# Ones stationary for row sums, a first root in two parts, ScalarE's high parts ahead of gate copies, and feed-forward matmuls of 512 columns

## The chip, the core and the metric

The kernel runs on one core of a Trainium2 chip. TensorE (PE) multiplies out of SBUF into PSUM, which has 8 banks of 128 partitions by 512 fp32 values; VectorE (DVE) and ScalarE (ACT) do the elementwise work; SyncE (SP) issues the transfers of the weights. Each engine runs its own instructions in order and waits on semaphores for the others. The metric is the device time of one execution in microseconds (us).

## The reference

The network has two blocks of two layers each, on 256 tokens of width 1024, all in fp32. Only what bears on the change is shown.

```python
# first block, layers i = 0 (differential attention with 256 context tokens) and 1 (short convolution)
mod = (silu_c @ ada_w[i] + ada_b[i])[:, None, :]          # 1024 -> 6 * 1024: six "sections" of a layer
sh1, sc1, g1, sh2, sc2, g2 = jnp.split(mod, 6, axis=-1)
h = modulate(rmsnorm(x, norm1_g[i]), sh1, sc1)             # x * (1 + scale) + shift
x = x + g1 * mixer(h)
x = x + g2 * swiglu(modulate(rmsnorm(x, norm2_g[i]), sh2, sc2), ffn_w_in[i], ffn_w_out[i])

def swiglu(t, w_in, w_out):                                # w_in: 1024 x 5632, w_out: 2816 x 1024
    a, b = jnp.split(t @ w_in, 2, axis=-1)
    return (silu(a) * b) @ w_out

# differential attention, per head of 8 (values of width 128), ends with
o = rmsnorm(o, subln_g) * (1.0 - lam_init)                 # over the 128 values of a head
return o.reshape(B, n, D_MODEL) @ wo
```

The second block (neighbourhood attention, then latent attention, each with a gated residual) is computed in the same program. Of it the change moves one instruction of ScalarE.

## The kernel before

**High and low parts.** A product of fp32 accuracy is made of three matmuls of the faster type fp32r: high weights by high input, high weights by low input, low weights by high input. Weights come in units of 1 MB (`raw`, a ring of 3 buffers). For each unit ScalarE rounds `raw` to `high` (`prepare`, L585) and VectorE subtracts to get `low` (`split`, L998). `behind(u)` on either engine makes the parts of unit u + 3: ScalarE's waits until PE is done with unit u (`blocks_done`), VectorE's waits for ScalarE's.

**Feed-forward phases** (`ffn_phase`, one for each layer of the first block). There are 11 steps of 256 hidden features. A step has two feature units (`two_features`, L1710, L1711, L1729), one for a and one for b, and one out unit (`out_unit`, L1625 to L1627) for the hidden features of the step before. The input is `hH`, `hL` (high and low part of x times scale, not yet divided by the root of the mean square), of 256 tokens and 2 columns that hold the shift, so a feature unit is 16 pairs of a 128x258 matmul with `hH` and one with `hL`, and 16 with the low weights. VectorE multiplies the result by `rstd` (`scaled`, L1242); the shift's column is added in ScalarE's silu (L726) and VectorE's `gated` (L1262). Then follow `gH` on ScalarE and `gL` on VectorE, which the next out unit needs.

**Adaptive sections.** The 12 sections of `mod` take rows of `ada_w` times silu(c). The first two are summed on PE (L1811, four column groups of 32 at once) and turned to columns with a selecting matmul (L1828). For the other ten, VectorE accumulates pieces of 128x1024 into `ada_acc` (L977), and PE sums over the partitions with 8 matmuls, `ada_acc` stationary and one column of ones moving (L1648). `reduce_at` holds after which unit each stands. VectorE's `section` then adds the bias. The first stands between two units of the q projection, the next two around the v projection, four in the first feed-forward phase, two in the convolution phase (behind its third and its last feature unit) and one in the second feed-forward phase.

**Attention's end.** Each of 16 (token tile, head) pairs is scored, exponentiated, transposed and multiplied with V; VectorE scales the result into `XN` (L1190) and ScalarE squares it (L691). When all 16 are squared, VectorE makes one root of 16 columns (`inverse_root`), scales four parts of `XN` (L1198), PE transposes them (`output_groups`), ScalarE makes `oH` (L606) and VectorE `oL` (L1045), and only then does the output product (`feature_out`) begin.

**Convolution phase.** Four times three feature units (c, u, g). ScalarE waits for VectorE's `tc`, copies it with its shift to `cg` (L746), and makes the high parts of the next units behind that. In the feed-forward phases silu stands ahead of the high parts in the same way.

## Time and profile before

| what | value |
|---|---|
| three runs | 1091.9, 1090.09, 1090.65 us; median 1090.65 |
| the profiled execution | 1092.87 us |
| its span (first to last instruction) | 1090.8 us |
| mean granted TensorE clock | 0.982 of 2.4 GHz |
| PE matmul busy | 1035.3 us (95%), 7740 instructions |
| DVE busy | 790.3 us (72%) |
| ACT busy | 509.4 us (47%) |
| chain that ended last | PE 79%, DVE 12%, ACT 3% |

Busy time counts a matmul from its start to its modelled end, and successive matmuls overlap; how fast they follow one another is read from their starts. The second block begins near 724 us. The first feed-forward phase runs from about 236 to 430 us, the convolution phase from 436 to 517 us and its output product to 542 us, the second feed-forward phase from there to about 735 us.

### The profile page before, as it was taken

Reading aid. Unit: us, or ns where it says so; the run is one execution under the profiler, and the core shown is the slowest. Engines: PE = TensorE matmul, PEld = TensorE weight load, DVE = VectorE, ACT = ScalarE, POOL = GpSimd, SP = SyncE. Lnnn points to the kernel's source line nnn. Section 1 sums busy time; section 2 is a strip of 40 time slices with the busy share of each in tenths; the row PEclk is TensorE's granted clock in tenths of the full one; section 3 lists DMA queues with packets and bytes.
Section 4 is the critical chain, followed back from the end, with each engine's and each line's share of the span. In section 5 each row is a group of like instructions: output and inputs, shape, how many; then the busy total and the mean of one; then the engine's idle time right before and its main releaser. Section 6 shows DMA issues by size and latency. Waiting matters only on the chain.

```text
span 1090.8 us, 18302 instructions
## 1 busy us (share of the span) xinstructions
PE 1035.3 (95%) x7740; PEld 960.9 (88%) x7740; DVE 790.3 (72%) x1184; ACT 509.4 (47%) x732; POOL 0.7 (0%) x6
## 2 busy tenths in 40 slices
PE   4899999799999999998999999999999999999895
PEld 2689875699999999998999999999987998997684
DVE  3689759668787887887986646568746568896665
ACT  3623238454434344424343444445347665457562
POOL 0000000000000000000000000000000000000000
PEclk9899999899999999999999999999999999999898
DMA  9769541038998987566746676564754053543130
GB/s 367 273 214 330 187 174 39 2 104 291 318 302 293 316 284 245 189 226 233 248 155 209 208 242 213 175 191 129 232 182 162 2 184 119 185 138 150 37 119 38
DMA packets 118592, 210.14 MB, mean 193 GB/s; under 512 B 4250, under 2 KB 82288, under 8 KB 118512
## 3 DMA queue, kind: packets, MB, share of 16 engines
q1 hardware_dynamic: 117764, 206.81, 55.9%
q10 hardware_dynamic: 748, 2.18, 0.5%
q8 instruction: 61, 1.00, 0.4%
q14 instruction: 19, 0.16, 0.1%
HBM read 207.92 MB, written 1.05 MB: 192 GB/s over the span
## 4 chain that ended last, share of the span: by engine, by line
PE 79%; DVE 12%; ACT 3%; issue 2%; DMA 1%; SPq 1%; DVEq 0%; ACTq 0%
PE PS L1625 12%; PE PS L1626 12%; PE PS L1627 12%; PE PS L1710 8%; PE PS L1729 8%; PE PS L1711 8%; DVE low L998 3%; PE PS L1636 3%; PE PS L1748 2%; PE PS L1749 2%; PE PS L1753 2%; PE PS L1843 1%; PE PS L1844 1%; DMA ada_raw<-in_ada_w 1%; PE PS L1916 1%
## 5 line engine op out<-in xcount | busy, mean ns | idle before, releaser
L998 DVE TENSOR_TENSOR low<-raw,high 128x2048 fp32r<-128x2048 f32 (+2 forms) x147 | 328.1, 2233 | 153.5 <-ACT high L585 153.1
L585 ACT ACTIVATE high<-raw 128x2048 fp32r<-128x2048 f32 (+2 forms) x147 | 273.1, 1866 | 226.0 <-PE PS L1627 111.2
L1710 PE MATMUL PS<-hH,high 128*128 128x258 f32 x896 | 221.8, 284 | 4.6 <-ACT high L585 1.9
L1711 PE MATMUL PS<-hL,high 128*128 128x258 f32 x896 | 220.3, 283 | 0.0
L1710 PEld LDWEIGHTS PS<-hH,high 128*128 128x128 f32 x896 | 169.8, 189 | 6.5 <-issue 2.9
L1711 PEld LDWEIGHTS PS<-hL,high 128*128 128x128 f32 x896 | 168.7, 188 | 0.1
L1729 PE MATMUL PS<-hH,low 128*128 128x258 f32 x896 | 126.3, 283 | 0.3
L1729 PEld LDWEIGHTS PS<-hH,low 128*128 128x128 f32 x896 | 115.6, 189 | 1.3 <-DVE low L998 1.3
L1625 PE MATMUL PS<-gH,high 128*128 128x256 f32 x352 | 98.5, 280 | 0.0
L1626 PE MATMUL PS<-gL,high 128*128 128x256 f32 x352 | 98.4, 280 | 0.0
L1627 PE MATMUL PS<-gH,low 128*128 128x256 f32 x352 | 98.2, 279 | 0.0
L977 DVE SCALAR_TENSOR_TENSOR ada_acc<-ada_raw,cond,ada_acc 128x1024 f32<-128x1024 f32 x70 | 89.6, 1281 | 4.9 <-DMA ada_raw<-in_ada_w 2.6
L1625 PE MATMUL PS<-oH,high 128*128 128x256 f32 x256 | 74.7, 292 | 1.8 <-issue 1.8
L1627 PE MATMUL PS<-oH,low 128*128 128x256 f32 x256 | 74.1, 289 | 0.0
L1626 PE MATMUL PS<-oL,high 128*128 128x256 f32 x256 | 73.9, 289 | 0.0
L726 ACT ACTIVATE sil<-ta,shifts 128x256 f32<-128x256 f32 x44 | 20.0, 502 | 110.8 <-DVE ta L1242 110.8
L1625 PEld LDWEIGHTS PS<-gH,high 128*128 128x128 f32 x352 | 66.2, 188 | 0.2 <-DVE gL L1269 0.2
L1627 PEld LDWEIGHTS PS<-gH,low 128*128 128x128 f32 x352 | 66.0, 187 | 0.0
L1626 PEld LDWEIGHTS PS<-gL,high 128*128 128x128 f32 x352 | 66.0, 187 | 0.0
L1625 PEld LDWEIGHTS PS<-oH,high 128*128 128x128 f32 x256 | 50.4, 197 | 2.9 <-issue 2.6
L1626 PEld LDWEIGHTS PS<-oL,high 128*128 128x128 f32 x256 | 50.3, 196 | 0.0
L1627 PEld LDWEIGHTS PS<-oH,low 128*128 128x128 f32 x256 | 50.1, 196 | 0.0
(325 smaller groups left out, 1945.8 us busy)
## 6 DMA issues: line engine op xcount, KB each, us to landing
raw<-in_ffn_w_in SPq DMA_DIRECT2D x44, 1024.0 KB, 6.4
ada_raw<-in_ada_w SPq DMA_DIRECT2D x82, 512.0 KB, 5.4
raw<-in_ffn_w_out SPq DMA_DIRECT2D x22, 1024.0 KB, 6.0
raw<-in_na_w_in SPq DMA_DIRECT2D x16, 1024.0 KB, 5.5
raw<-in_da_wqkv SPq DMA_DIRECT2D x12, 1024.0 KB, 8.8
raw<-in_sc_w_in SPq DMA_DIRECT2D x12, 1024.0 KB, 5.7
raw<-in_ple_w_gate SPq DMA_DIRECT2D x8, 1024.0 KB, 4.8
raw<-in_mla_w_in SPq DMA_DIRECT2D x7, 1024.0 KB, 5.4
```

Source lines behind the costliest of these rows:

```text
L585: nc.scalar.activation(high[s][:, 0:width(u)], raw[s][:, 0:width(u)], ACT.Copy).then_inc(high_ready, 1)
L977: V_.scalar_tensor_tensor(acc[:, :], ada_raw[p % RING][:, :], cond[:, k, 0:1], acc[:, :], ALU.mult, ALU.add).then_inc(ada_used_dve, 1)
L998: V_.tensor_tensor(low[s][:, 0:w], raw[s][:, 0:w], high[s][:, 0:w].bitcast(F), ALU.subtract).then_inc(low_dve, 1)
L1625: MM(o, wH, xH, start=start, stop=False, skip_group_check=shared)
L1626: MM(o, wH, xL, start=False, stop=False, skip_group_check=shared)
L1627: return MM(o, wL, xH, start=False, stop=stop, skip_group_check=shared)
L1636: last = nc.tensor.transpose(PS[0:n, b, c:c + w], src, ident[0:w, 0:w])
L1710: MM(PS[:, b + c, 0:SEQ + 2], high[s][w(j, c)], hH[:, j, 0:SEQ + 2], start=j == 0, stop=False)
L1711: MM(PS[:, b + c, 0:SEQ + 2], high[s][w(j, c)], hL[:, j, 0:SEQ + 2], start=False, stop=False)
L1729: last = MM(PS[:, b + c, 0:SEQ + 2], low[s][w(j, c)], hH[:, j, 0:SEQ + 2], start=False, stop=j == KC - 1)
L1748: MM(o(c), high[s][w(j, c)], hH[:, j, 0:SEQ], start=j == 0 and c == 0, stop=False, skip_group_check=True)
L1749: MM(o(c), high[s][w(j, c)], hL[:, j, 0:SEQ], start=False, stop=False, skip_group_check=True)
```

## The change

Seven things are changed, in the same file.

1. **Paired features.** From step 3 of 11 on (`PAIRED = 3`), the input of a feature unit is the finished, scaled and shifted input of the layer, high part `oH` and low part `oL`, now two halves of one tile `oHL`. One matmul of 512 columns takes both against a high weight; one of 256 columns takes the low weight against `oH` and adds into the first half. VectorE sums the halves with a reduction (`both_parts`). To make `oHL`, VectorE multiplies XT by `rstd` at the end of step 0, ScalarE scales and shifts 8 chunks and rounds at the end of step 1, and VectorE subtracts.
2. **Row sums.** The ten later sections are summed with ones stationary (32 columns) and `ada_acc` moving, in four column groups; ScalarE copies the row out (`copy_rows`), and PE turns it with two transposes (`turn_rows`) one unit later; VectorE's part (`section_turned`) follows that.
3. **First two sections.** 16 transposes of `ada_acc` in place of 16 selecting matmuls; VectorE adds the four partial rows with a reduction.
4. **Root in two parts.** The root of the first 12 columns is made between the last three heads, two scalings stand ahead of the last head's result, and the last four columns and the fourth group of transposes come later, the group behind the first output unit.
5. **High parts first.** In the feed-forward phases ScalarE makes the high part of the next unit ahead of silu.
6. The same ahead of the gate copy in the convolution phase.
7. In the latent attention, the high part of the gated heads stands ahead of the exponentials.

```diff
+            def paired_features(u, b):
...
+                pe.wait_ge(high_ready, u + 1)
+                for c in range(2):
+                    claim(b + c)
+                    for j in range(KC):
+                        MM(bank(b + c), high[s][w(j, c)], oHL[:, :, j, :], start=j == 0, stop=False, skip_group_check=True)
+                    if c == 0:
+                        unit_ready(u)
+                    for j in range(KC):
+                        last = MM(bank(b + c, SEQ), low[s][w(j, c)], oH[:, j, :], start=False, stop=j == KC - 1, skip_group_check=True)
+                    last.then_inc(blocks_done, 1)
...
+            def both_parts(dst, b):
+
+                return V_.tensor_reduce(dst[:, :, :], PS[:, b:b + 2, :].rearrange("p c (h n) -> p c n h", h=2), AX.X, ALU.add)
...
+                    if i == 0:
+                        V_.tensor_tensor(paired[:, :, :], XT[:, :, :], rstd[:, :].unsqueeze(1).to_broadcast([P, KC, SEQ]), ALU.mult).then_inc(paired_scaled, 1)
+                    if i == 1:
+                        seen.next(paired_high)
+                        V_.tensor_tensor(oL[:, :, :], paired[:, :, :], oH[:, :, :].bitcast(F), ALU.subtract).then_inc(paired_low, 1)
...
             def behind(u):
 
+                turn_rows()
                 if u not in reduce_at:
                     return
                 g = reduce_at[u]
                 pe.wait_ge(ada_used_dve, KC * (g - 1))
                 claim(7)
-                owed(section_taken, 7)
-                for c in range(KC):
-                    last = MM(PS[:, 7, c:c + 1], ada_acc[g % 2][:, c * P:(c + 1) * P], ones[:, 0:1], start=True, stop=True)
-                last.then_inc(section_made, 1)
+                for j in range(4):
+                    last = MM(PS[32 * j:32 * j + 32, 7, 0:SEQ], ones[:, 0:32], ada_acc[g % 2][:, j * SEQ:(j + 1) * SEQ],
+                              start=True, stop=True, tile_position=(0, 32 * j))
+                last.then_inc(rows_made, 1)
+                owed(rows_copied, 7)
+                turning.append(u)
...
+                if i == 13:
+                    v.wait_ge(sq_ready, 12)
+                    link(V_.tensor_scalar(var[:, 0:12], ssq[:, 0:12], 1.0 / P, EPS, ALU.mult, ALU.add))
+                    root_guess(var[:, 0:12], rst[:, 0:12], nwt[:, 0:12])
+                if i == 14:
+                    root_series(nwt[:, 0:12], poly[:, 0:12])
+                if i == 15:
+                    root_closed(rst[:, 0:12], nwt[:, 0:12], poly[:, 0:12])
+                    da_scaled(0, 0)
+                    da_scaled(1, 0)
                 seen.next(made_v)
...
+            da_scaled(0, 1)
+            da_low(0, 0)
+            da_low(1, 0)
             v.wait_ge(sq_ready, 16)
-            inverse_root(0, 16, P)
...
+            inverse_root(12, 16, P)
+            da_scaled(1, 1)
+            da_low(0, 1)
+            da_low(1, 1)
...
                 u = first["sc_in"] + 3 * j
+                behind(u)
                 seen.next(c_taken)
                 for c in range(2):
                     ins = nc.scalar.activation(cg[:, c, :], tc[:, c, :], ACT.Identity, bias=shifts[:, c:c + 1])
                 ins.then_inc(c_copied, 1)
-                behind(u)
...
+                if p % 2 == 0 and p:
+                    gated_high(p // 2 - 1)
                 if p + 2 < 8:
                     exps(2 * p + 4, False)
                     exps(2 * p + 5, False)
-                if p % 2 == 0 and p:
-                    gated_high(p // 2 - 1)
```

How the order of instructions moves is shown at three places; the names are those of the program's tiles.

PE in a feed-forward phase: one block of 128 features of a unit. Before, the end of such a block and the section behind its unit read:

```order
L1710 MATMUL PS<-hH,high 128x258
L1711 MATMUL PS<-hL,high 128x258
L1729 MATMUL PS<-hH,low 128x258 x8
L1648 MATMUL PS<-ones,ada_acc 128x1 x8
L1710 MATMUL PS<-hH,high 128x258
```

In the changed kernel the same place (step 3, both blocks of the a unit, the section, the b unit, the turning of the section's row, the out unit) reads:

```order
L1854 MATMUL PS<-oHL,high 128x512 x8
L1858 MATMUL PS<-oHL,low 128x256 x8
L1854 MATMUL PS<-oHL,high 128x512 x8
L1858 MATMUL PS<-oHL,low 128x256 x8
L1754 MATMUL PS<-ada_acc,ones 32x256 x4
L1854 MATMUL PS<-oHL,high 128x512 x8
L1858 MATMUL PS<-oHL,low 128x256 x8
L1854 MATMUL PS<-oHL,high 128x512 x8
L1858 MATMUL PS<-oHL,low 128x256 x8
L1730 MATMUL PS<-ident,wide 128x128 x2
L1719 MATMUL PS<-gH,high 128x256
```

Each pair of matmuls with `hH` and `hL` has become one of 512 columns; the section is now four matmuls here and two transposes a unit later.

ScalarE in the convolution phase. Before, a gate copy and then three high parts:

```order
L746 ACTIVATE cg<-tc,shifts 128x256 x2
L585 ACTIVATE high<-raw 128x2048 x3
L752 ACTIVATE oH<-cf 128x512
```

In the changed kernel one high part stands ahead of the gate copy and two behind it, and where a section is due its row is copied out (L608):

```order
L599 ACTIVATE high<-raw 128x2048
L780 ACTIVATE cg<-tc,shifts 128x256 x2
L599 ACTIVATE high<-raw 128x2048 x2
L786 ACTIVATE oHL<-cf 128x512
```

VectorE at the attention's end. Before, behind the last two heads' results (`XN` from PSUM):

```order
L1190 TENSOR_SCALAR XN<-PS,rsum 128x128 x2
L1013 TENSOR_SCALAR var<-ssq 128x16
L1022 TENSOR_SCALAR rst<-var 128x16
```

In the changed kernel, from the 15th head's result on:

```order
L1270 TENSOR_SCALAR XN<-PS,rsum 128x128
L1084 SCALAR_TENSOR_TENSOR poly<-poly,nwt 128x12 x2
L1085 SCALAR_TENSOR_TENSOR rst<-poly,rst 128x12
L1240 TENSOR_TENSOR XN<-XN,rst 128x512 x2
L1270 TENSOR_SCALAR XN<-PS,rsum 128x128
L1240 TENSOR_TENSOR XN<-XN,rst 128x512
L1103 SCALAR_TENSOR_TENSOR oHL<-PS,cols,oHL 128x4x128 x2
L1060 TENSOR_SCALAR var<-ssq 128x4
```

The root of 12 columns and two scalings stand ahead of the last head's result, and the root of the last four behind the first two low parts.

## Rows read from the trace of the kernel before

**Rows 1.** The page: busy us (share of the span) and instructions of each engine.

```profile
PE 1035.3 (95%) x7740; PEld 960.9 (88%) x7740; DVE 790.3 (72%) x1184; ACT 509.4 (47%) x732; POOL 0.7 (0%) x6
```

**Rows 2.** The chain that ended last, feed-forward phase: start us, us, what.

```profile
267.75 0.96 PE PS L1729 x8
270.63 0.96 PE PS L1729 x8
...
284.94 0.97 PE PS L1729 x8
...
325.17 1.68 PE PS L1648 x16
```

**Rows 3.** The same chain, matmuls of 512 and of 256 columns.

```profile
60.19 3.63 PE PS L1861 x16
...
745.70 1.90 PE PS L1753 x16
747.60 1.75 PE PS L1762 x8
...
1066.63 1.75 PE PS L1636 x16
```

**Rows 4.** The same chain at the start: the two first sections.

```profile
30.07 1.92 PE PS L1811 x16
31.99 4.40 PE PS L1828 x32
```

**Rows 5.** Timeline of the start: start, us, row, [idle before it].

```profile
39.01 0.77 PE L1843 MATMUL PS<-dH,high 128*128 128x512 f32 x1 [2.62 <-DVE dL L1111]
```

**Rows 6.** Windows: us, busy by engine, PEclk (granted clock), DMA share, GB/s.

```profile
44.00:45.00 1.00, 1.00 (x4) 0.81 (x3) 1.00 (x1) 1.00 (x3) 0.00 (x0) 0.52 0.00 0
...
206.00:207.00 1.00, 0.00 (x0) 0.00 (x0) 0.83 (x6) 0.00 (x0) 0.00 (x0) 0.50 0.00 0
...
518.00:520.00 2.00, 2.00 (x11) 2.00 (x11) 1.93 (x5) 0.17 (x1) 0.00 (x0) 0.50 0.95 266
```

**Rows 7.** Timeline at the attention's end: PE, ACT, DVE.

```profile
207.74 3.67 PE L1636 MATMUL PS<-ident,XN 128*128 128x128 f32 x16 [3.70 <-DVE XN L1198]
...
211.27 0.58 PE L1625 MATMUL PS<-oH,high 128*128 128x256 f32 x1
...
217.75 1.92 ACT L585 ACTIVATE high<-raw 128x2048 fp32r<-128x2048 f32 x1 [5.61 <-PE PS L1627]
...
204.89 0.17 DVE L1013 TENSOR_SCALAR var<-ssq 128x16 f32<-128x16 f32 x1 [0.47 <-ACT rope_T L691]
...
206.99 2.50 DVE L1198 TENSOR_TENSOR XN<-XN,rst 128x512 f32<-128x512 f32 x4
209.61 3.31 DVE L1045 SCALAR_TENSOR_TENSOR oL<-PS,cols,oH 128x512 fp32r<-128x512 f32 x4
```

**Rows 8.** Timeline of the convolution phase's last two turns: DVE and PE.

```profile
494.76 2.29 DVE L998 TENSOR_TENSOR low<-raw,high 128x2048 fp32r<-128x2048 f32 x1 [2.78 <-ACT high L585]
...
514.60 2.29 DVE L998 TENSOR_TENSOR low<-raw,high 128x2048 fp32r<-128x2048 f32 x1 [2.78 <-ACT high L585]
...
538.62 0.88 DVE L1207 SCALAR_TENSOR_TENSOR XT<-PS,mod,XT 128x256 f32<-128x256 f32 x2
...
517.00 0.55 PE L1625 MATMUL PS<-oH,high 128*128 128x256 f32 x1 [1.79 <-issue]
```

**Rows 9.** DVE by line and form, one step (329 to 346 us) and over the span (L1166).

```profile
L998 DVE TENSOR_TENSOR low<-raw,high 128x2048 fp32r<-128x2048 f32 x3 | 6.9, 2289 | 2.7 <-ACT high L585 2.7
...
L1242 DVE TENSOR_TENSOR ta<-PS,rstd 128x512 f32<-128x512 f32 x1 | 0.7, 681 | 0.0
...
L1166 DVE TENSOR_REDUCE nmax<-PS 128x2 f32<-128x1024 f32 x16 | 19.4, 1219 | 3.0 <-PE PS L1882 3.0
```

**Rows 10.** Window of the same step: busy PE, PEld, DVE, ACT; clock; DMA share; GB/s.

```profile
329.00:346.00 17.00, 17.00 (x144) 17.00 (x144) 14.51 (x13) 6.47 (x7) 0.00 (x0) 1.00 0.92 308
```

**Rows 11.** Timeline of the latent attention: PE.

```profile
1023.57 1.08 PE L2206 MATMUL PS<-PT,V 128*64 128x256 f32 x8 [2.60 <-ACT PT L910]
```

More of the change, by code:

```diff
@@ L588, in behind, with copy_rows @@
                 prepare(u + RING)
+            def copy_rows(u):
+                if u in reduce_at:
+                    seen.next(rows_made)
+                    nc.scalar.activation(sum_rows[:, :], bank(7, SEQ), ACT.Copy).then_inc(rows_copied, 1)
             def square(src, col, junk, scale=1.0):
@@ L664, in _ @@
                 behind(first["da_q"] + j)
+                copy_rows(first["da_q"] + j)
             def da_exp(i):
@@ L736, in ffn_phase @@
                         behind(ua + 2)
-            ffn_phase(first["ffn0"])
+                    if i == 1:
+                        seen.next(paired_scaled)
+                        for c in range(KC):
+                            ins = nc.scalar.activation(paired[:, c, :], paired[:, c, :], ACT.Identity,
+                                                       scale=mod[:, scale, c:c + 1], bias=mod[:, shift, c:c + 1])
+                        ins.then_inc(act_step, 1)
+                        seen.next(act_step)
+                        nc.scalar.activation(oH[:, :, :], paired[:, :, :], ACT.Copy).then_inc(paired_high, 1)
+            ffn_phase(first["ffn0"], SCALE2, SHIFT2)
             close(first["sc_in"] - 1, 6 + SCALE1, 6 + SHIFT1)
@@ L978, in piece, with section, section_turned @@
                                             ALU.mult, ALU.add).then_inc(ada_used_dve, 1)
-            def section(g):
+            turning = []
+            def section(u):
+                turning.append((reduce_at[u], rows_bank(u, first)))
+            def section_turned():
+                if not turning:
+                    return
+                g, b = turning.pop()
                 layer, part = divmod(g, 6)
@@ L1637, in transposes, with turn_rows @@
                 return last
+            turning = []
+            def turn_rows():
+                if not turning:
+                    return
+                b = rows_bank(turning.pop(), first)
+                seen.next(rows_copied)
+                claim(b)
+                transposes(b, [(h * P, P, sum_rows[:, h * P:(h + 1) * P]) for h in range(2)]).then_inc(section_made, 1)
+                owed(section_taken, b)
             def behind(u):
+                turn_rows()
                 if u not in reduce_at:
@@ L1821, in _ @@
             for g in range(2):
[L1822 to L1828 removed]
+                for n in range(2):
+                    b = 4 + 2 * g + n
+                    pe.wait_ge((acc_copied, acc_half)[n], g + 1)
+                    claim(b)
+                    last = transposes(b, [(c * P, P, ada_acc[g][:, (4 * n + c) * P:(4 * n + c + 1) * P]) for c in range(4)])
                 last.then_inc(section_made, 1)
[L1830 removed]
+                owed(section_taken, b - 1, b)
             for half in range(2):
```

128 lines of the change are left out of this document (86 added, 42 removed).

## The prediction

> **What bounds the kernel now.** The first view is the page's list of engines: PE is busy 1035.3 us of the span, 95%, DVE 72%, ACT 47% [rows 1]. So a change can gain in two ways: fewer or shorter matmuls where PE runs without a gap, or a shorter wait where it does not. The chain of waits tells these places apart. In the feed-forward phases it runs through PE alone: 24 matmuls of 258 columns take 2.88 us (270.63 less 267.75), 0.120 us each, and a step of 144 takes 17.19 us (284.94 less 267.75) [rows 2]. There, what counts is the number of matmuls and their spacing. The timelines show where PE waits: at the attention's end for 3.70 us [rows 7], ahead of the convolution's output product for 1.79 us [rows 8], in the latent attention for 2.60 us [rows 11]. Behind the first two of these, and at the start, the granted clock stands at 0.50 (1.2 GHz) for some us, though PE works again [rows 6].
>
> **Paired features.** Two layers have 8 paired steps each, two units a step: 32 units. A unit was 48 matmuls in 5.77 us. It becomes 16 of 512 columns and 16 of 256. Sixteen of 512 took 3.63 us, 0.227 each; sixteen of 256 in a row took 1.90 us, 0.119 each [rows 3]. Together 5.53 us, so a unit gains 0.24. What is saved is not columns but the spacing that comes on top of them, which a 512 pays once and two 258s twice. 32 units give 7.4 us. What the trace doesn't show is a moving operand made of two strips of 256 that lie apart; I take the rate of the unbroken one. Bounds: nothing gained, or 8.5 if the low matmuls also run at the 0.118 of the out units (17.19 less 4 times 2.88, over 48).
>
> By the Trainium skill (TensorE: Matmul & The Clock Gate, Back-to-back issue gap) a warm matmul follows the last at N/2.4 plus about 2.5 ns. That is 110 ns for 258 columns and 216 for 512, where the rows show 120 and 227. By the page a unit would gain 0.08 us and the term would be 2.6 us, not 7.4. The rows decide here: the spacing above N/2.4 is 12 to 13 ns in both.
>
> **What VectorE pays.** `scaled` of 0.68 us becomes a reduction of 1024 values from PSUM; the nearest row is the 1219 ns of L1166 [rows 9], which has the same input but one output for 512. A step has two: 1.1 us more, less about 0.4 for the shifts' copy and for `gated` in one piece. In a step of 17 us DVE is busy 14.5 [rows 10], and its wait of 2.7 us for ACT's high part [rows 9] fills the rest. Item 5 takes most of this wait away, since the high part no longer waits for silu. So DVE needs about 15.2 plus 0.7 of wait in a step that shrinks to 16.7: it still fits, PE stays the bound. If a reduction took 2.0 us, a step would need 17.5 and DVE would set the pace. Making `oHL` costs DVE twice 2.29 us (the form of L998 [rows 8]) and ACT 8 times 0.5 plus 1.9, in steps 0 to 2, once a layer. Behind them on DVE wait `ta` of step 2 and the splits. The bank of `ta` is asked for by PE a whole step later, and `oL` comes some 4 us ahead of step 3, so I count nothing; without this cover it would be 4.6 us a layer. DMA is at 0.92 of its engines in this phase [rows 10] at 308 GB/s, and 3% more is asked; weights have the time of two units to spare.
>
> **Row sums.** A section takes PE 1.68 us now (16 instructions, two for each fp32 matmul) [rows 2]. Four column groups of 512 columns ran together: 8 matmuls in 1.92 us [rows 4]; four of 256 have a quarter of that work, 0.48. Two transposes cost 0.11 each [rows 3]. I add 0.15 to 0.2 for the change from full array to groups and back: 0.9, a gain of 0.8. Bounds: 0.70 (gain 1.0), and the groups in series, 1.75 as L1762 [rows 3], plus 0.22, a loss of 0.3. ACT's copy (0.4 us) and the second half of the work come one unit, 5.5 us, later than the first, so PE doesn't wait for it. DVE's part waits behind `gated`, where PE has long turned the row. Eight of the ten sections stand in stretches without a gap: 6.4 us. The other two are in the convolution phase and are in its term.
>
> **The start.** The 16 selecting matmuls took 4.40 us [rows 4]. Sixteen transposes at 0.12 are 1.9 us, but the second eight need a copy that lands near 32.7, so they end near 34.0 instead of 36.4. DVE has two more small reductions, 0.25 each. The first product therefore starts 1.9 us ahead of 39.01 [rows 5]. Its matmuls ran at the lower clock, still 0.52 at 44 to 45 [rows 6]; if the clock rises as soon after the first of them as before or a little sooner, 2.3 us are gained. Bounds: 1.0 (the clock rises at the same moment, so the head start is worth half) and 3.0.
>
> **The attention's end.** Now: last product ends at 204.0, root from 204.89, scalings from 206.99, transposes 207.74 to 211.27, output product from 211.27, its first unit done at 217.75 [rows 7]. After: the root's steps for 12 columns lie in DVE's gaps of the last three heads, 0.6 to 0.8 us a head, and two scalings (0.62 each) just fit ahead of the last result at 204.0. PE turns three groups until 205.6; ACT squares the last head until 204.9 and makes two high parts until 206.2; DVE's two low parts of 0.8 end near 207.2. The first output unit runs from there to 212.9. The second root (nine small steps, 2.1 us) and the fourth scaling end at 210, under this unit, and the fourth group of transposes costs 0.5 behind it: 213.4 instead of 217.75, so 4.3. I take 4.2. If the clock falls to 0.50 all the same [rows 6], half of it is lost: 2.1.
>
> **The convolution phase.** Here DVE is the bound: its turn takes 19.84 us (514.60 less 494.76), of which 2.78 is the wait for the high part; a wait of this size stands in each of the four turns [rows 8]. PE needs 17.3 for three units (6 times 2.88). With the high part ahead of the gate copy it is ready when `tc` is done, the wait is gone, and a turn takes 17.1 to 17.7: DVE and PE nearly level. Four waits are 11.1 us, by which the sum that starts the close, at 538.62 [rows 8], comes earlier. PE must follow: it loses its own stalls, two times 0.8 from the sections, the 1.79 us ahead of 517.00 and the half clock behind it until after 522 (0.213 against 0.118 us each, 27 matmuls, 2.6 us) [rows 6, 8], with its stalls of some 5 us within the phase 11 in all. I take 11.0. Next late would be the low part of the third output unit, within 0.6 us of its need. Bounds: 8 and 11.5.
>
> **The latent attention.** The high part of the gated heads ran behind four exponentials; DVE stood on it twice and PE then for 2.60 us [rows 11]. Ahead of them it is ready before DVE asks. I take 2.0; bounds 0.5 and 2.6.
>
> **The sum.** 7.4 + 6.4 + 2.3 + 4.2 + 11.0 + 2.0 = 33.3 us. The profiled execution took 1092.87; this gives 1059.6 for one like it. It lies 2.2 above the median of the three runs, 1090.65, from which the forecast is 1057.
>
> **Rivals.** (a) The low clock keeps its hold: at the start and the attention's end the transposes and short waits leave the clock low longer. That takes 1.3 and 2.1, perhaps 1 at the convolution: 1061.5. For it: it was low at each of the three places. Against it: PE's idle time there falls from 3.7 to some 1.6 us. The Trainium skill (the same page, PE-mode transpose) holds that transposes don't count as work for the clock, which would do this at the first two places. The rows show no case of transposes alone.
> (b) The reduction costs DVE 2.0 us or more, since it writes 512 results with strided reads. DVE then paces the first feed-forward phase, 0.8 us in each of 8 steps, of which little hides: 1063. For it: no row has this form. Against: the same input in 1.22.
> (c) The paired matmul saves only the page's 0.08 us a unit or the two strips cost some ns: 1062.
> (d) The column groups don't run together with ones stationary: 1.1 us more for ten sections, 1068. Against: L1811 shows them together.
> (e) Slower than before: a moving operand of two strips streams slower. There are 512 such matmuls; from 0.227 plus 0.065, that is 0.292 us each, the 33.3 us are gone, and at half rate the kernel would take some 1170. No row has such an operand; the two strips are each unbroken runs of 256, which speaks against it.
> (f) The waits that were removed were not what held PE in the convolution phase, because DVE's pieces then wait for their DMA: half of the 11 is lost, 1063.
>
> **Chances.** The forecast as it stands (1053 to 1060) 0.57; (a) 0.12; (b) 0.08; (c) 0.09; (d) 0.03; (f) 0.06; (e) 0.02; no gain for another reason 0.03. The range from 1052 to 1066 takes in all but (d), (e), the last, and the worst of (b) and (f). This kernel's measurement tells 0.2%, about 2.2 us, from no change. Faster 0.95, same 0.02, slower 0.03.
>
> **What would show it.** Right: L1854's 512-column matmuls 0.227 us apart and a paired step of 16.7; a section of 0.9 on PE; no wait of 2.8 at DVE's splits in the convolution; the output product at 207; no half clock at 517. Wrong: reductions of 2 us, PE waiting for `a_taken` or `hid_low`, clock low at 207 to 213.

## The result, and the profile after

The changed kernel takes 1057.74 us (median of 4 runs, 1057.16 to 1058.77), the kernel before, measured beside it, 1091.07: a ratio of 0.9696, 95% interval 0.9679 to 0.9713, or 33.3 us less. The forecast was 1057.0 with a range of 1052 to 1066. The profiled execution took 1058.77, its span is 1057.0.

The page of the changed kernel, busy us (share of the span) and instructions of each engine, against [rows 1]:

```profile
PE 1010.4 (96%) x7152; PEld 910.3 (86%) x7152; DVE 814.1 (77%) x1167; ACT 521.1 (49%) x744; POOL 0.7 (0%) x6
```

PE has 588 instructions less and 24.9 us less to do; VectorE has 23.8 us more, and its share rises from 72 to 77%.

That the total came out within 1 us says nothing yet about the terms. Points that both chains pass show where the time went. Each time is the start of the same row in either chain, and the third column is how much of the lead was won in the stretch that ends there.

| point in the chain of waits | before | after | won in this stretch | forecast |
|---|---|---|---|---|
| first low product of 16 matmuls | 49.31 | 47.81 | 1.50 | 2.3 |
| values of the last head (8 matmuls of 1.17) | 202.88 | 200.47 | 0.91 | 2.4 (three sections) |
| scaling for the first feed-forward phase (ACT XN x8, 2.56) | 236.42 | 229.68 | 4.33 | 4.2 |
| the same for the convolution phase | 437.22 | 423.21 | 7.27 | 6.9 (four sections, 16 pairs) |
| the same for the second feed-forward phase | 544.48 | 518.89 | 11.58 | 11.0 |
| first projection of the second block | 739.98 | 710.67 | 3.72 | 4.5 (one section, 16 pairs) |
| first head pair of the latent attention | 994.98 | 966.14 | -0.47 | 0 |
| last transposes | 1066.63 | 1032.79 | 5.00 | 2.0 |

Together 33.8 us; behind the last point nothing moves by more than 0.02. Two stretches miss by more than 1 us, the second and the last, in opposite directions.

**A paired step.** The chain of the changed kernel in the first feed-forward phase (start, us, what), against [rows 2, 3]:

```profile
281.85 0.57 PE PS L1754 x8
282.42 2.05 PE PS L1854 x8
284.47 0.95 PE PS L1858 x8
285.42 1.86 PE PS L1854 x8
287.28 0.95 PE PS L1858 x8
288.23 0.22 PE PS L1730 x2
```

The row sums take 0.57 us, the two transposes 0.14 to 0.22, and the first paired block behind the sums 0.18 more than the others (2.05 against 1.87). With the smaller transitions (the units on both sides of the sums 5.71 to 5.73 for 5.62, the output unit behind the transposes 5.69 to 5.74 for 5.60) a section costs PE 1.0 us. Before it was 1.70 and 0.08 behind it, 1.78. So 0.79 are gained, where the forecast had 0.8. Eight matmuls of 512 columns take 1.865 us, that is 0.233 each and not 0.227; eight of 256 take 0.945, 0.118 each. A unit takes 5.62 us for 5.77: 0.15 gained, where the forecast had 0.24.

**VectorE in such a step.** DVE by line and form, 329 to 346 us, against [rows 9]; and the window of a whole paired step, 294 to 310.8 us, columns as in [rows 10]:

```profile
L1044 DVE TENSOR_TENSOR low<-raw,high 128x2048 fp32r<-128x2048 f32 x3 | 6.9, 2289 | 1.4 <-ACT high L599 1.4
...
L1325 DVE TENSOR_REDUCE ta<-PS 128x512 f32<-128x1024 f32 x1 | 1.2, 1223 | 0.1
```

```profile
294.00:310.80 16.80, 16.80 (x114) 15.39 (x114) 16.66 (x13) 7.05 (x6) 0.00 (x0) 1.00 1.00 343
```

The reduction costs 1.22 us although it writes 512 results: rival (b) is out. But the cover is thin in places: VectorE was busy 16.66 of these 16.80 us, in the fullest of the steps from 294 us on. The next one took 14.05, and the mean of seven such steps is 14.9 (104.28 us busy in 294 to 411.6), where the prediction had 15.2:

```profile
310.80:327.60 16.80, 16.80 (x116) 14.83 (x115) 14.05 (x13) 7.18 (x6) 0.00 (x0) 1.00 0.89 298
```

**The attention's end.** PE's timeline of the changed kernel, against [rows 7]:

```profile
201.46 1.04 PE L1730 MATMUL PS<-ident,XN 128*128 128x128 f32 x8
202.67 0.66 PE L1730 MATMUL PS<-ident,XN 128*128 128x128 f32 x4 [0.17 <-DVE XN L1240]
204.52 0.39 PE L1719 MATMUL PS<-oHL,high 128*128 128x256 f32 x1 [1.20 <-DVE oHL L1103]
```

The wait of 3.70 us has shrunk to 0.17 and 1.20. The output product starts 2.9 us behind the last head's values (201.64) where it was 7.2, and the granted clock stays at 1.00 through 212 us.

**The convolution phase.** VectorE's timeline in its last turn, against [rows 8]:

```profile
494.15 2.29 DVE L1044 TENSOR_TENSOR low<-raw,high 128x2048 fp32r<-128x2048 f32 x1
...
514.41 0.88 DVE L1286 SCALAR_TENSOR_TENSOR XT<-PS,mod,XT 128x256 f32<-128x256 f32 x2 [0.39 <-PE PS L1721]
```

The wait of 2.78 ahead of the split is gone in all four turns (442.11, 459.68, 477.18, 494.15: turns of 17.57, 17.50 and 16.97 us for 19.84 before), and the close's sum stands at 514.41 for 538.62. PE runs its units of this phase without a gap.

### The profile page after: what moved, and what is told of

Read it like the earlier page. It is cut to its first block, busy times and chain, and to the rows that moved or that the text cites. A ratio compares the mean times of both kernels' runs of the same rounds, so it can differ in the third digit from the quotient of the medians.

```text
span 1057.0 us, 17136 instructions
## 1 busy us (share of the span) xinstructions
PE 1010.4 (96%) x7152; PEld 910.3 (86%) x7152; DVE 814.1 (77%) x1167; ACT 521.1 (49%) x744; POOL 0.7 (0%) x6
## 4 chain that ended last, share of the span: by engine, by line
PE 85%; DVE 8%; ACT 2%; DMA 2%; SPq 1%; issue 1%; DVEq 0%; ACTq 0%
PE PS L1719 12%; PE PS L1721 12%; PE PS L1720 12%; PE PS L1854 11%; PE PS L1858 6%; PE PS L1820 4%; PE PS L1839 3%; PE PS L1821 3%; PE PS L1730 3%; DVE low L1044 2%; PE PS L1877 2%; PE PS L1878 2%; PE PS L1882 2%; DMA raw<-in_da_wqkv 2%; PE PS L2044 2%; PE PS L1970 2%
## 5 line engine op out<-in xcount | busy, mean ns | idle before, releaser
L1854 PE MATMUL PS<-oHL,high 128*128 128x512 f32 x512 | 129.9, 395 | 0.0
L1854 PEld LDWEIGHTS PS<-oHL,high 128*128 128x128 f32 x512 | 91.9, 188 | 18.7 <-issue 1.6
L1820 PE MATMUL PS<-hH,high 128*128 128x258 f32 x384 | 95.5, 285 | 1.0 <-DVE ta L1321 0.5
L1821 PE MATMUL PS<-hL,high 128*128 128x258 f32 x384 | 94.5, 284 | 0.0
L1820 PEld LDWEIGHTS PS<-hH,high 128*128 128x128 f32 x384 | 72.7, 189 | 2.7 <-issue 1.7
L1858 PEld LDWEIGHTS PS<-oHL,low 128*128 128x128 f32 x512 | 69.5, 188 | 5.8
L1719 PE MATMUL PS<-oHL,high 128*128 128x256 f32 x256 | 72.6, 284 | 1.2 <-DVE oHL L1103 1.2
L1821 PEld LDWEIGHTS PS<-hL,high 128*128 128x128 f32 x384 | 72.3, 188 | 0.1
L1721 PE MATMUL PS<-oHL,low 128*128 128x256 f32 x256 | 72.0, 281 | 0.0
L1720 PE MATMUL PS<-oHL,high 128*128 128x256 f32 x256 | 72.0, 281 | 0.0
L1858 PE MATMUL PS<-oHL,low 128*128 128x256 f32 x512 | 71.1, 281 | 0.0
L1839 PE MATMUL PS<-hH,low 128*128 128x258 f32 x384 | 53.7, 283 | 0.0
L1719 PEld LDWEIGHTS PS<-oHL,high 128*128 128x128 f32 x256 | 48.2, 188 | 2.2 <-DVE oHL L1103 1.4
```

The lines of the kernel that those rows point to most:

```text
L1719: MM(o, wH, xH, start=start, stop=False, skip_group_check=shared)
L1720: MM(o, wH, xL, start=False, stop=False, skip_group_check=shared)
L1721: return MM(o, wL, xH, start=False, stop=stop, skip_group_check=shared)
L1820: MM(PS[:, b + c, 0:SEQ + 2], high[s][w(j, c)], hH[:, j, 0:SEQ + 2], start=j == 0, stop=False)
L1821: MM(PS[:, b + c, 0:SEQ + 2], high[s][w(j, c)], hL[:, j, 0:SEQ + 2], start=False, stop=False)
L1839: last = MM(PS[:, b + c, 0:SEQ + 2], low[s][w(j, c)], hH[:, j, 0:SEQ + 2], start=False, stop=j == KC - 1)
```

## The experiments

Times are medians; "changed" is 1057.74. Ratios are to the kernel before, measured beside each group on the same chip, where its median was 1091.34 (the a runs), 1090.68 (b), 1091.79 (c) and 1091.14 (d). An interval of a ratio is 3 to 7 us wide, so differences of 1 or 2 us between two forms need a trace beside them.

**a1: the two strips joined.** The third rival, and the one behind it, put a price on a moving operand in two strips.

```diff
-        oHL = sb("oHL", [P, 2, KC, SEQ], R)
-        oH, oL = oHL[:, 0, :, :], oHL[:, 1, :, :]
+        oHL = sb("oHL", [P, KC, 2, SEQ], R)
+        oH, oL = oHL[:, :, 0, :], oHL[:, :, 1, :]
...
-                        MM(bank(b + c), high[s][w(j, c)], oHL[:, :, j, :], ...)
+                        MM(bank(b + c), high[s][w(j, c)], oHL[:, j, :, :], ...)
```

> The changed kernel with the high and low parts of a feature side by side in memory (256 high, 256 low, then the next feature), so that the paired matmul's moving operand is one unbroken run of 512; the q and k parts that lie over the same memory are laid out likewise. In the changed kernel these matmuls stand 0.233 us apart, unbroken ones 0.227. Theory 1: the two strips cost the 6 ns; then the 512s stand 0.227 apart, a paired unit falls from 5.62 to 5.52 us, and 32 units give 3.2 us: about 1054.5. Theory 2: the 6 ns come from something else in this block (what is stationary, the bank, the turn from 512 to 256 columns); then nothing moves by more than 0.5 us.

Measured: 1057.34 us, ratio 0.9689 (0.9674 to 0.9703). The chain of this kernel:

```profile
582.02 1.86 PE PS L1854 x8
584.83 1.87 PE PS L1854 x8
```

Still 0.233 each. The strips cost nothing; theory 2 holds.

**a2: no pairs.**

```diff
-PAIRED = 3
+PAIRED = 11
```

> The changed kernel with all eleven steps of both feed-forward phases unpaired, as before the change; the copies that fill the paired operand are still made. Theory 1: pairing saves 0.145 us a unit (two units in 11.24 us against 11.53), so 32 units cost 4.6 us: about 1062.4. Theory 2: the step's other shortening, 5.60 for an output unit against 5.66, comes from pairing too; then 5.5 to 6 us, 1063.5. If the forecast's 0.24 a unit were right after all, 1065.

Measured: 1062.36 us, ratio 0.9731 (0.9717 to 0.9746), 4.6 us more than the changed kernel. The two feed-forward stretches of the table take 195.79 and 194.40 us in its chain, against 193.53 and 191.81 in a1's: 2.3 and 2.6 for 16 units each. Pairing is worth 0.15 us a unit, as theory 1 has it. An output unit takes 5.60 here too, so that its shortening doesn't come from pairing.

**a3: 8 bytes where the selecting matrix was.**

```diff
         ones = sb("ones", [P, P])
+        pad = sb("pad", [P, 2])
```

> The changed kernel with 8 unused bytes a partition where the removed selecting matrix stood, so that all later buffers lie where they lay before. Theory 1: the place of gH, gL and ml_aH in memory sets their matmuls' spacing; then an output unit in the feed-forward phase goes back from 5.60 to 5.66 us and the latent projection's spacing from 0.120 to 0.117 us: 1.2 us lost in one, 0.6 gained in the other, 1058.4. Theory 2: the place has nothing to do with it: spacings stay as in the changed kernel.

Measured: 1056.80 us (1055.95 to 1058.55), ratio 0.9688 (0.9671 to 0.9705), no difference that can be told. Its timeline at one output unit of the feed-forward phase, from the unit's first row to the first of the next, and then the same in the changed kernel:

```profile
302.44 0.28 PE L1720 MATMUL PS<-gH,high 128*128 128x256 f32 x1
...
308.10 0.63 PE L1855 MATMUL PS<-oHL,high 128*128 128x512 f32 x2
```

```profile
305.16 0.28 PE L1719 MATMUL PS<-gH,high 128*128 128x256 f32 x1
...
310.76 0.62 PE L1854 MATMUL PS<-oHL,high 128*128 128x512 f32 x2
```

5.66 us against 5.60. In the second block three matmuls with `ml_aH` and `ml_aL` as moving operands take 0.350 us with the 8 bytes, as before the change, and 0.360 without. So theory 1 holds for the spacings: by taking away a matrix of 8 bytes a partition, the change moved all buffers behind it. It won 0.06 us in each of 22 output units; of this 0.39 and 0.32 us show in the two feed-forward stretches (193.92 and 192.10 us in a3). It lost 0.47 in the second block, whose stretch in the table takes 255.00 us before, 255.47 in the changed kernel and 254.98 in a3. The total of 1058.4 that theory 1 gave was off. The traced execution lies 2.6 us below the changed kernel's, and this is the start's: it kept the full clock there (2.9 us, see d1). Whether the other three did isn't shown.

**a4: the gate copy first again.** The order of ScalarE in a convolution turn as before the change.

```diff
                 u = first["sc_in"] + 3 * j
-                behind(u)
                 seen.next(c_taken)
                 for c in range(2):
                     ins = nc.scalar.activation(cg[:, c, :], tc[:, c, :], ACT.Identity, bias=shifts[:, c:c + 1])
                 ins.then_inc(c_copied, 1)
+                behind(u)
```

> The changed kernel with ScalarE's gate copy ahead of the high part again in each of the four convolution turns, as before. Theory 1: the wait of 2.8 us at VectorE's split comes back four times and with it the half clock behind the phase: 10 to 11.6 us, about 1069. Theory 2 (rival): the order alone is worth less, since the sections' shorter stops in this phase and the earlier arrival did part of it: 5 to 8 us, 1064.

Measured: 1068.34 us, ratio 0.979 (0.9776 to 0.9805), 10.6 us more. VectorE's timeline and a window of this kernel:

```profile
438.76 2.29 DVE L1044 TENSOR_TENSOR low<-raw,high 128x2048 fp32r<-128x2048 f32 x1 [2.78 <-ACT high L599]
...
499.33 2.29 DVE L1044 TENSOR_TENSOR low<-raw,high 128x2048 fp32r<-128x2048 f32 x1 [2.78 <-ACT high L599]
```

```profile
502.00:504.00 2.00, 2.00 (x11) 2.00 (x11) 1.96 (x4) 1.16 (x2) 0.00 (x0) 0.50 0.64 119
```

All four waits are back, and the half clock behind the phase too. One instruction's place on an engine that is busy half the time is a third of the whole gain.

**b1: sums by column again.**

```diff
-                for j in range(4):
-                    last = MM(PS[32 * j:32 * j + 32, 7, 0:SEQ], ones[:, 0:32], ada_acc[g % 2][:, j * SEQ:(j + 1) * SEQ],
-                              start=True, stop=True, tile_position=(0, 32 * j))
-                last.then_inc(rows_made, 1)
+                for c in range(KC):
+                    last = MM(PS[:, 7, c:c + 1], ada_acc[g % 2][:, c * P:(c + 1) * P], ones[:, 0:1], start=True, stop=True)
+                last.then_inc(section_made, 1)
```

(ScalarE's copy and the two transposes are left out, and VectorE reads the column from bank 7.)

> The changed kernel with the ten sections summed as before: 8 matmuls with one column of ones moving, no copy and no transposes. Theory 1: a section costs PE 1.78 us in place of 1.0 (as read behind units of the two traces), so nine sections in stretches that PE bounds and one more give 0.79 each: 7.9 us, about 1065.5. Theory 2 (rival): in the convolution phase, where VectorE is nearly level with PE, and around the v projection part of it hides: 5 to 6 us, 1063.

Measured: 1066.34 us, ratio 0.9769 (0.9739 to 0.9798), 8.6 more; theory 1, a little above. Some of it isn't the sections' own cost on PE: the two feed-forward stretches are 3.90 and 1.61 us longer for four sections and one, 0.7 and 0.8 more than 0.79 each, and in both PE waited once for VectorE's `mod` (0.4 and 0.5 us). And in one place this kernel is faster. Windows (PE, PEld, DVE, ACT, POOL, granted clock, DMA share, GB/s) in the attention's first heads, of the changed kernel and then of b1:

```profile
165.00:166.00 1.00, 1.00 (x7) 0.30 (x4) 0.98 (x3) 0.65 (x2) 0.00 (x0) 1.00 0.99 342
166.00:167.00 1.00, 1.00 (x5) 0.71 (x4) 0.95 (x3) 1.00 (x5) 0.00 (x0) 0.55 1.08 382
167.00:168.00 1.00, 1.00 (x7) 1.00 (x6) 1.00 (x2) 0.68 (x3) 0.00 (x0) 0.50 0.77 255
```

```profile
167.00:168.00 1.00, 1.00 (x5) 0.24 (x5) 0.96 (x4) 0.88 (x3) 0.00 (x0) 1.00 1.01 353
168.00:169.00 1.00, 1.00 (x11) 1.00 (x10) 0.96 (x3) 1.00 (x5) 0.00 (x0) 1.00 1.08 383
```

In the changed kernel the granted clock falls to 0.50 behind a wait of PE for `gates` and stays there until 169. Before the change PE waited as long at the same place and the clock stayed at 1.00, as it did in b1. The two waits, changed and before:

```profile
164.58 0.66 PE L1730 MATMUL PS<-ident,gates 128*128 128x128 f32 x4 [1.72 <-DVE gates L1234]
```

```profile
168.55 0.66 PE L1636 MATMUL PS<-ident,gates 128*128 128x128 f32 x4 [1.72 <-DVE gates L1174]
```

What differs ahead of the wait is the section, with its 1.68 us of PE work before and 0.57 and two transposes now. From the first low product to the last head's values the changed kernel takes 152.66 us and b3, which has the same sections but in its profiled execution no such fall, 151.10: the fall costs 1.56 us. It is there in ten of the eleven traces with the new sums and in none of the three with the old. So it goes with the new sums, but b3, with the same sections and the same wait of 1.72 us, shows that they don't bring it every time; what else decides is open.

**b2: the root in one piece.**

```diff
-                if i == 13:
-                    ...
-                if i == 15:
-                    root_closed(rst[:, 0:12], nwt[:, 0:12], poly[:, 0:12])
-                    da_scaled(0, 0)
-                    da_scaled(1, 0)
...
-            da_scaled(0, 1)
-            da_low(0, 0)
-            da_low(1, 0)
             v.wait_ge(sq_ready, 16)
-            inverse_root(12, 16, P)
-            da_scaled(1, 1)
-            da_low(0, 1)
-            da_low(1, 1)
+            inverse_root(0, 16, P)
+            for t, b in BY_HALF:
+                da_scaled(t, b)
+            for t, b in BY_HALF:
+                da_low(t, b)
...
-            output_groups(xn_ready, BY_HALF[:3])
+            output_groups(xn_ready, BY_HALF)
```

> The changed kernel with the attention's first root, scalings and turns in one piece behind the last head, as before. Theory 1: the wait of 3.7 us and the four groups of transposes ahead of the output product come back whole: 4.3 us, about 1062. Theory 2 (rival): the half clock would hold the output product back in either form, so that only half is lost: 2.1 us, 1060.

Measured: 1061.45 us, ratio 0.9725 (0.969 to 0.9759), 3.7 more. In its timeline PE waits as before:

```profile
202.17 3.42 PE L1718 MATMUL PS<-ident,XN 128*128 128x128 f32 x16 [3.69 <-DVE XN L1240]
205.45 0.58 PE L1707 MATMUL PS<-oHL,high 128*128 128x256 f32 x1
```

From the last head's values to the next scaling its chain takes 33.09 us, the changed kernel's 29.21: 3.9 us. The median agrees: theory 1.

**b3: the gated heads' high part behind the exponentials.**

```diff
-                if p % 2 == 0 and p:
-                    gated_high(p // 2 - 1)
                 if p + 2 < 8:
                     exps(2 * p + 4, False)
                     exps(2 * p + 5, False)
+                if p % 2 == 0 and p:
+                    gated_high(p // 2 - 1)
```

> The changed kernel with the high part of the gated heads behind the exponentials again in the latent attention. Theory 1: VectorE's two waits and PE's wait of 2.6 us come back, and so does the half clock at the start of the output product, which the changed kernel's trace doesn't show: 4.5 us, about 1062. Theory 2: only the 2.0 us that the prediction gave it: 1059.7.

Measured: 1059.86 us (1058.94, 1059.22, 1060.50, 1062.90), ratio 0.9714 (0.9682 to 0.9747). The median is 2.1 us above the changed kernel, the profiled execution (1062.90) 4 to 5. Its windows, and below them the changed kernel's at the same place:

```profile
994.00:996.00 2.00, 2.00 (x10) 1.28 (x7) 0.01 (x1) 0.13 (x1) 0.00 (x0) 0.50 0.00 0
...
1000.00:1002.00 2.00, 2.00 (x11) 2.00 (x10) 2.00 (x2) 1.88 (x2) 0.00 (x0) 0.50 0.00 0
```

```profile
994.00:996.00 2.00, 1.26 (x12) 0.90 (x12) 0.00 (x0) 1.60 (x3) 0.00 (x0) 1.00 0.00 0
997.00:999.00 2.00, 2.00 (x19) 2.00 (x18) 2.00 (x2) 1.89 (x3) 0.00 (x0) 1.00 0.00 0
```

In the profiled execution the clock fell behind PE's wait of 2.60 us, as it did in the profiled execution before the change (0.50 at 1029 to 1031). The two parts can be told apart in the traces. The product behind that wait, in b3 and in the changed kernel:

```profile
992.81 1.98 PE L2345 MATMUL PS<-PT,V 128*64 128x256 f32 x8 [2.60 <-ACT PT L944]
```

```profile
992.69 1.08 PE L2345 MATMUL PS<-PT,V 128*64 128x256 f32 x8 [1.70 <-ACT PT L944]
```

It starts 28.59 us behind the first head pair in b3, as it does before the change, and 26.55 in the changed kernel: the waits are worth 2.04 us. From there to the last transposes b3 takes 44.12 us, the kernel before 43.06 and the changed kernel 40.10: the low clock cost 4.0 and 3.0 us more. That b3's profiled execution is only 4 to 5 us above the changed kernel is because it had no fall of the clock in the first heads (1.56). The spread of the four times suggests that the clock doesn't fall in every execution; a profile exists of one only. So both theories have a part.

**b4: silu first again in the feed-forward steps.**

```diff
                     copy_rows(ua)
-                    behind(ua)
                     seen.next(a_taken)
...
                     ins.then_inc(silu_ready, 1)
+                    behind(ua)
```

> The changed kernel with ScalarE's silu ahead of the weight's high part again in the feed-forward steps. Theory 1: VectorE's wait of 2.7 us for that high part comes back; with the longer reductions a step of the first phase then needs 17.5 to 18 us of VectorE against 16.8 of PE, and the eight paired steps lose some 0.8 each: 6 to 8 us with the second phase untouched, about 1064. Theory 2 (rival): the wait is slack that other work of VectorE does not need; PE stays the bound and the time is 1057.7, with some 0.3 us either way.

Measured: 1071.59 us, ratio 0.9818 (0.9787 to 0.9848), 13.9 us more, twice what theory 1 gave. The first phase takes 206.8 us in its chain, the changed kernel's 193.5. The chain of b4 runs through the making of the paired operand:

```profile
264.52 1.90 ACT high L599
266.43 3.95 ACT XN L765 x8
...
270.40 1.92 ACT oHL L769
...
272.35 2.29 DVE oHL L1367
```

PE's units around it grow (an output unit 7.67 for 5.60, the two paired units 13.92 for 11.43): 4.6 us. At the phase's end the last two output units take 18.87 us for 11.21, 7.7 us more, with this wait for VectorE's low part between them:

```profile
426.49 0.58 PE L1719 MATMUL PS<-gH,high 128*128 128x256 f32 x1 [4.86 <-DVE gL L1358]
```

Behind it the granted clock stood at 0.50 from 426 to 432, with matmuls 0.21 us apart, which is most of the rest of the 7.7. Between opening and end a paired step without a section loses 0.4 to 0.7, one with a section nothing; the phase's close takes 1.1 less. The second phase loses 1.1. So VectorE doesn't merely set the pace: it falls behind, and its lateness comes out mostly where the phase opens and where it closes.

**c1 and c2: the paired operand moved by 8 and by 128 bytes.**

```diff
+        ahead = sb("ahead", [P, 2])     # c1; [P, 32] in c2
         with ExitStack() as s:
             nq = sb("na_qT", [P, KC, SEQ], F, s)
```

> The changed kernel with 8 unused bytes a partition ahead of the paired operand, so that it and all that lies behind it move by 8 bytes. Joined strips left its 512-column matmuls at 0.233 us; 8 bytes moved the spacing of the 256-column matmuls behind gH and ml_aH. Theory 1: the moving operand's place in memory sets the spacing; then the 512s change, to 0.227 at best (about 3 us less, 1054) or upward. Theory 2: the 0.233 has another cause and stays; the output units go back to 5.66 us, which alone gives 1058.5.

> The changed kernel with 128 unused bytes a partition ahead of the paired operand. Theory 1: if a coarse part of the place matters (128 bytes against the next multiple), the 512s change with this shift and not with 8 bytes: 0.227, about 1054.5. Theory 2: neither matters: 0.233, 1057.5, and the output units stay at 5.60 us, since their place changes by a multiple of 128 only.

Measured: c1 1057.63 us, ratio 0.969 (0.9673 to 0.9706); c2 1058.67 us, ratio 0.9696 (0.9682 to 0.9711). The 512-column matmuls stand 0.2341 us apart in c1 and 0.2305 in c2 (the mean of the 32 chain rows of eight in the second feed-forward phase; the changed kernel's is 0.2330). Rows of c2:

```profile
585.94 1.84 PE PS L1855 x8
588.73 1.84 PE PS L1855 x8
```

The place does act, by 1 to 3 ns, but no place tried brings the 0.227 of [rows 3], and in the total nothing of it can be told. The output units take 5.65 us in c1, near the 5.66 expected, and 5.63 to 5.64 in c2, where 5.60 was expected: a shift by 128 bytes acts on them too. What the rest of the 6 ns is stays open.

**c3: the kernel before with the high part ahead of silu, alone.** The edit is b4's in reverse, on the kernel before.

> The kernel before with one part of the change alone: ScalarE's high part ahead of silu in the feed-forward steps. In the changed kernel undoing this cost 13.9 us. Theory 1: it is cover, not gain: before, VectorE is busy 14.5 of 17 us and PE paces the phase, so the order alone gives nothing: within 0.7 us of the kernel before. Theory 2: it has a gain of its own, at the phase's start, where VectorE catches up: 1 to 3 us less.

Measured: 1088.00 us (10 runs), ratio 0.997 (0.9955 to 0.9985): 1.6 to 4.9 us less than before. Theory 2 holds. In the traces the first feed-forward stretch is 199.06 us for 200.80, the second is as long as before, and most of the 1.7 us is at the first one's end (the last two output units 11.30 for 12.04, the close's first unit 6.86 for 7.66). In the view of waits, VectorE's for the high part fall from 153.1 to 128.7 us in all.

**d1: the start with selecting matmuls.**

```diff
+        sel2 = esum[:, 0:2]
...
-                    last = transposes(b, [(c * P, P, ada_acc[g][:, (4 * n + c) * P:(4 * n + c + 1) * P]) for c in range(4)])
+                    last = MM(PS[:, b, 2 * c:2 * c + 2], ada_acc[g][:, c * P:(c + 1) * P], sel2, start=True, stop=True)
```

(VectorE reads the two columns of each feature from PSUM, without its reductions.)

> The changed kernel with the two first sections turned by the 16 selecting matmuls again, as before; the selecting matrix lies in memory that is free at that time, so that no buffer moves. In the two profiled executions the third low product started 1.5 us earlier after the change (47.81 against 49.31), but over seven executions of changed forms the same point lay between 44.65 and 47.81, as the clock rose sooner or later. Theory 1: the prediction's 2.3 us, and those two executions differ by less only by chance: 1059.8. Theory 2: the clock's rise sets the end of this stretch, and the head start of 1.3 us at the first product is all there is or less: 1057.7 to 1059.

Measured: 1058.71 us (5 runs), ratio 0.9701 (0.9688 to 0.9715), 1.0 more, within the interval of no difference. The chain of d1, and PE's timeline of the changed kernel, against [rows 4, 5]:

```profile
32.48 3.68 PE PS L1956 x32
```

```profile
32.27 1.98 PE L1730 MATMUL PS<-ident,ada_acc 128*128 128x128 f32 x16
37.67 0.77 PE L1970 MATMUL PS<-dH,high 128*128 128x512 f32 x1 [3.42 <-DVE dL L1171]
```

The first product starts at 38.77 in d1 and at 37.67 in the changed kernel, and yet the low product starts only 0.4 us apart (48.24, 47.81). The clock decides between: it is low from 36 to about 43 in both. Over the eleven executions with the new start the low product started between 44.65 and 47.81. Three of them (a3, b2, c1) kept the full clock through the start, as a3's window shows:

```profile
38.00:40.00 2.00, 2.00 (x10) 1.64 (x9) 1.97 (x5) 2.00 (x4) 0.00 (x0) 1.00 0.94 300
```

Theory 2: about 1 us, inside a spread of 3 that comes in the main from the clock (in b1 also from weights that landed 0.8 us later).

The 32 selecting matmuls took 3.68 us in d1 at the full clock. The 4.40 of [rows 4], from which the forecast was made, were read in an execution whose clock fell to 0.50 at 34.7 us, while they ran.

## Why the prediction was right, term by term

| term | forecast | by undoing it | by the two traces |
|---|---|---|---|
| paired features | 7.4 | 4.6 (a2) | 4.8 |
| ten sections | 8 (6.4 and two in the convolution's term) | 8.6 (b1) | 0.79 each, less 1.56 for the clock |
| the start | 2.3 | 1.0 (d1), not told from nothing | 1.5 |
| attention's end | 4.2 | 3.7 (b2) | 4.3 |
| convolution phase | 11.0 | 10.6 (a4, the order alone) | 11.6 |
| latent attention | 2.0 | 2.1 (b3) | 2.0, and 3.0 for the clock |
| high part ahead of silu | 0 | 13.9 (b4); 3.3 alone (c3) | about 1.2 (the rest of the first feed-forward stretch's 7.27); 1.7 in c3's |

By undoing, the terms with a forecast sum to 30.6 of the 33.3 us. c3's 3.3 (1.6 to 4.9) could close the rest; b4's 13.9 is no part of such a sum, since it is what the other items would lose without the cover. The mechanisms were those that the prediction named. That the total came out within 1 us is in part luck: sizes were off in both directions and nearly cancelled.

**Paired features: mis-sized.** The step was the rate of an unbroken 512-column matmul, 0.227 us from [rows 3]. It measured 0.233, which is 0.10 us a unit, and the gain 0.15 instead of 0.24. (32 units at 0.24 are 7.5 to 7.7 us, by the rounding, and not 7.4, and the upper bound, with the low matmuls at 0.118, comes to 8.1 and not 8.5; neither slip changes the reading.) The prediction's guess at what might do this, the two strips, is refuted by a1. The place in memory has a share (c2), the rest is open. Rival (c) was therefore half right: it priced the loss at 5 us, some 2.8 were lost, and the reason that it gave for the strips is wrong. By the Trainium skill (TensorE: Matmul & The Clock Gate, Back-to-back issue gap) the gap of isolated matmuls on the warm array is N/2.4 plus about 2.5 ns, which gives, as an estimate, 0.08 us a unit. The trace doesn't agree: the 0.15 measured lies between that and the rows' 0.24, and the spacing above N/2.4 was 20 ns here and 12 at the 256s.

**VectorE's cost: right, and closer to the edge than told.** The reduction took 1.22 us, as in the row that was chosen, and PE ran the paired steps without a wait. The sentence that item 5 takes the wait away and that VectorE "still fits" was the load-bearing one, and b4 shows its price: 13.9 us. Of these 4.6 lie around the making of the paired operand, as much as the prediction had put on it without its cover (4.6 us a layer), but in the first phase alone, where VectorE is near its limit. The step missed two things: that the same order would win 1.6 to 4.9 us by itself (c3), at the end of the phase, where a late VectorE had held PE all along, and that lateness adds up to the phase's close (7.7 us, of which 4.86 are the wait and most of the rest the half clock behind it) and is paid step by step only in small part.

**Row sums: right in price, incomplete in effect.** 0.9 was forecast for a section, 1.0 was read, against 1.78 and not 1.68. What no step had was the clock in the first heads: behind PE's wait of 1.72 us, which cost nothing more before, the clock fell, and 1.56 of the three sections' 2.4 us were given back. That the section's cut PE work let it fall is what ten of eleven traces against none of three suggest; b1 puts that work back and the clock holds, but b3 keeps it cut and the clock holds too. Rival (a) had the mechanism, but looked at the start and the attention's end. At the attention's end the clock held.

**The start: mis-sized.** The transposes ended at 34.25, forecast 34.0. The 4.40 us that they replaced were 3.68 at the full clock (d1), so that 0.7 of the head start came from the clock of one execution. But the first `dH` then waited 0.6 us for ScalarE, which had taken the weight's high part at 33.84 and was free at 35.66, so that the first product came at 37.67 and not at 37.1 (the row sums ahead of it were 0.35 later than before, too); and the clock rose at its own time. The Trainium skill (the same page, PE-mode transpose) holds that transposes don't count as work for the clock in the same way. Here 16 transposes in place of 32 selecting matmuls left the clock's fall at 36 as it was in d1, and in three executions there was no fall at all, so that no run shows such an effect.

**The attention's end and the convolution phase: right.** The output product started 2.9 us behind the last head's values, forecast 3.2. The turns were 17.0 to 17.6 us, forecast 17.1 to 17.7. a4 puts 10.6 of the 11.6 us on the order of two ScalarE instructions, so that rival (f), a DMA behind the wait, is out.

**Latent attention: the wait right, the clock missed.** The 2.0 is what the traces show for the wait (2.04) and the medians for the edit (2.1). In the profiled execution before, the clock had also fallen behind this wait, to 0.50 until 1031.4, and the prediction didn't read that stretch's clock. This is the excess of 3.0 us in the table's last row.

## What to carry to other kernels

An engine that is busy half its time can still hold the kernel: a high part that VectorE and TensorE both wait for belongs ahead of a copy that only its neighbour reads, and where the cover is thin the order is worth more than the edit that it covers (10.6 and 13.9 us here, against 4.6 for the wider matmuls). When work is taken from PE just ahead of a wait, read the granted clock behind the wait, since the part that was saved may have been what kept it up. Before a row is used as a price, read the clock at which it was taken. And test a term by undoing it alone even when the total came out: here several sizes were wrong by 1 to 3 us and nearly cancelled.

## What the runs showed of the hardware

- The spacing of matmuls depended on where the moving operand lies in memory. 8 bytes more or less ahead of `gH` and `gL` gave 5.66 or 5.60 us for 48 matmuls of 256 columns, and ahead of `ml_aH` and `ml_aL` 0.350 or 0.360 us for three. For the paired operand, 128 bytes gave 0.2305 for 0.2330 us at 512 columns. No rule was found.
- A moving operand of two runs of 256 that lie apart streamed as fast as one of 512 (0.233 us in both).
- A reduction over pairs with a stride, 1024 fp32 values of PSUM to 512, took 1.22 us on VectorE, as long as the same input reduced to 2 results [rows 9].
- The clock at the start isn't the same in every execution of nearly the same program: full throughout in three of the eleven forms with the new start, at 0.50 for 3 to 7 us in the others. The first low product started up to 3.2 us apart.
- A wait of PE of 1.72 us left the clock at 1.00 in the three traces with 1.68 us of column sums on PE some us ahead of it, and was followed by 0.50 for 3 to 4 us in ten of the eleven with 0.57.
